# A norm's root moved behind the input products of a two-layer mixer, and the turn of rows by column halves

## Chip, cores and metric

The kernel runs on one core of a Trainium2 chip. The metric is the device time of one execution in microseconds (us), lower is better; 0.2% is 4 us.

## The reference, cut to what matters

Two blocks follow each other on 256 tokens of width 1024, all in float32. The first (layer norms, a state space mixer with attention, a mixture of 16 experts) ends in a layer norm with gain and bias. The second has two layers, and each of them begins so:

```python
def rmsnorm(x, g):
    x32 = x.astype(jnp.float32)
    y = x32 * lax.rsqrt(jnp.mean(x32 * x32, axis=-1, keepdims=True) + NORM_EPS)
    return (y * g.astype(jnp.float32)).astype(x.dtype)
...
# in each layer: h = rmsnorm(x, norm_mix); proj = h @ w_in  (2744 columns for
# three kinds of attention, then 3072 for the gates, which pass a sigmoid)
# ... attention, gates, products, cross attention, x = x + ...
# then x = x + w_down(silu(gate) * up), the feed-forward part with 2816 columns
```

The factor of the root is one number for each token, so it can be applied to the normed row or to the row of the product; both give the same `h @ w_in`.

## The kernel before, in words

Tokens lie on the 128 partitions in two blocks (`TB` = 2), `x_rows` holds them. A product needs its left side turned, so 128x128 tiles are transposed by TensorE (PE) with an identity into two PSUM banks X and O, two tiles `k` of two token blocks in one bank (`turn_rows`, L577; the transpose is L586). Most weights are used at a higher precision than one pass gives: a value is split into a rounded high part and a low part, and a product is made of three passes, high by high, high by low and low by high (`passes`, L599). For a chunk of weights ScalarE (ACT) writes the high part (`make_high`, L1346, the copy is L1353) and VectorE (DVE) subtracts it in place (`make_low`, L1665, L1669). For the turned tiles ACT writes the high part with the norm's gain (`turned_high`, L1355, L1362), and DVE writes the whole tile `h_t` (L1655), which the gate products read, and the low part (L1657).

All weights come through a ring of three places in SBUF (`SLOTS` = 3, a place holds 2 MB). SyncE (SP) issues the loads in the order of `LAYER_CHUNKS` (`load`, L1179, the issue is L1202); chunk number j goes to place j mod 3, and its load waits until PE has used the chunk before it in that place. A layer has 41 chunks and one `unused` behind them. It begins with `in1, in0, in2, in3, in4, in5` (the columns of the attention part; `in1` has 256 columns, `in4` and `in5` 476, the others 512), then the gates `g0` to `g5` among others; it ends with `gu0` to `gu10` (feed-forward, gate and up) and `fd0` to `fd5` (down; `fd5` is half a chunk). `in0` and `in2` are loaded in 16 pieces each, since their columns are put in another order on the way (pairs of heads, `PAIRED`).

The order of work is written by hand for each engine and held together by semaphores; each engine runs its own program in order. At the start of a layer:

```python
rms_rows("layer", "mix", ...)         # DVE: var, wait for GpSimd's root, x_rows * root -> h_rows (L1674, L1677)
turn_rows("mix", [... h_rows ...])    # PE: 8 tiles, two banks, so tiles 4 to 7 wait for 0 to 3
for i in IN_ORDER:                    # PE: product of both token blocks, banks G0 and G1
    product_rows("layer", f"in{i}", ...)
```

ACT computes the sums of squares for it (`square_rows`, L1341, two 128x1024 operations) as soon as `x_rows` is whole, GpSimd (POOL) takes the root (L1288), DVE scales the rows. ACT takes each product out of PSUM (`take`, L1331, L1339) into `proj`. DVE rotates the queries and keys (L2199 to L2209).

The turn into layer 0 comes behind the last product of the experts: DVE adds, norms and scales the rows (L2021, L1684 to L1701, the last two are the gain and the bias of the layer norm on 128x2048), and then the start above follows. The turn into layer 1 comes behind `fd5` of layer 0: PE's down product (L1128) runs over k, for each k over token block and column half, so both banks S and PT are full only at its end; DVE adds half of them to `x_rows` (L2456, two of 128x1024). At the start of each layer ACT issues eleven small loads (gains, position vectors, sinks, L1497 to L1502), PE turns the gains onto the partitions (L948) and DVE copies them (L2181).

## Time and profile before

| | |
|---|---|
| three runs | 1970.43, 1973.97, 1972.98 us; median 1972.98 |
| profiled execution | 1971.96 us, its span 1970.2 us |
| PE busy | 1755.8 us (89%), mean granted clock 0.932 |
| DVE, ACT, POOL busy | 853.9, 593.7, 22.6 us (43, 30, 1%) |
| DMA | 333.24 MB, mean 169 GB/s |

The profile is of one execution. A granted clock of 1.00 is 2.4 GHz, one of 0.50 is 1.2 GHz. `Ln` is a line of the kernel before. `ring_r`, `early_w` and `late_w` are the low part and the high parts of weights, `mix_high` and `mix_low` those of the turned tiles. "issue" in a chain is time in which an engine waited for nothing that the profile shows. The end of a row is its start plus its duration.

### The profile page before, as it was taken

What the parts mean: (1) busy time and instruction counts of PE and PEld (TensorE: products, weight loads), DVE (VectorE), ACT (ScalarE), POOL (GpSimd) and SP (SyncE); (2) the same over time, 40 slices, a digit from 0 to 9 for tenths busy, and PEclk for the clock granted to TensorE, in tenths of its full rate; (3) what the DMA queues carried; (4) which work ended last, traced back from release to release, by engine and by line L of the source; (5) the groups of instructions that cost most, each with busy time, mean ns of one, the idle gap of its engine ahead of it and who ended that gap; (6) DMA issues with size and microseconds to landing.
All of it is one profiled execution on the core that took longest, in us unless ns stands there. A gap on an engine that the chain in (4) does not pass through costs nothing.

```text
span 1970.2 us, 21742 instructions
## 1 busy us (share of the span) xinstructions
PE 1755.8 (89%) x9183; PEld 1284.4 (65%) x9183; DVE 853.9 (43%) x1201; ACT 593.7 (30%) x879; POOL 22.6 (1%) x80
## 2 busy tenths in 40 slices
PE   5999899988999959999988779996999989859997
PEld 1997555454434328565677679985756667649995
DVE  4675153243101055353465345534543365434643
ACT  1443210000111123243434234423333533433341
POOL 1000010000000000000000000000000000000000
PEclk9899787988999979999989889997999998979998
DMA  7455222657999964413234135536433232414552
GB/s 242 170 179 201 91 86 85 219 193 292 400 401 405 405 137 165 152 44 128 107 128 171 43 129 172 204 118 151 167 107 110 99 140 105 167 43 154 189 178 90
DMA packets 211212, 333.24 MB, mean 169 GB/s; under 512 B 51251, under 2 KB 102709, under 8 KB 211125
## 3 DMA queue, kind: packets, MB, share of 16 engines
q1 hardware_dynamic: 205312, 325.90, 47.5%
q10 hardware_dynamic: 5814, 6.11, 0.9%
q8 instruction: 65, 1.06, 0.2%
q14 instruction: 21, 0.17, 0.0%
HBM read 330.94 MB, written 1.05 MB: 168 GB/s over the span
## 4 chain that ended last, share of the span: by engine, by line
PE 68%; issue 12%; DVE 8%; DMA 7%; ACT 4%; SPq 1%; POOL 0%; POOLq 0%; DVEq 0%; ACTq 0%
PE ps_g L611 20%; PE ps_g L626 12%; PE ps_g L991 7%; DMA arena<-in_w_up_dram 5%; PE ps_g L911 4%; PE ps_o L681 3%; PE ps_p L611 2%; PE ps_s L611 2%; DMA ring<-in_w_mod_dram 2%; PE ps_p L1128 2%; PE ps_s L1128 2%; PE ps_s L652 1%; DVE ring_r L1669 1%; PE ps_x L586 1%; PE ps_p L671 1%
## 5 line engine op out<-in xcount | busy, mean ns | idle before, releaser
L1669 DVE TENSOR_TENSOR ring_r<-ring,late_w 128x4096 fp32r<-128x4096 f32 (+1 forms) x52 | 225.8, 4343 | 153.5 <-ACT late_w L1353 153.5
L1353 ACT ACTIVATE late_w<-ring 128x4096 fp32r<-128x4096 f32 (+1 forms) x52 | 185.0, 3557 | 234.7 <-PE ps_g L626 111.5
L626 PE MATMUL ps_g<-h_t_r,late_w 128*128 128x256 f32 x768 | 219.0, 285 | 0.0
L626 PE MATMUL ps_g<-hf_high,late_w 128*128 128x256 f32 x704 | 199.0, 283 | 3.8 <-DVE h_t_r L1657 3.8
L626 PE MATMUL ps_g<-hf_high,ring_r 128*128 128x256 f32 x704 | 199.0, 283 | 0.0
L626 PEld LDWEIGHTS ps_g<-h_t_r,late_w 128*128 128x128 f32 x768 | 148.6, 193 | 0.0
L991 PE MATMUL ps_g<-ring,h_t 128*128 128x512 f32 x320 | 145.7, 600 | 0.0
L626 PEld LDWEIGHTS ps_g<-hf_high,late_w 128*128 128x128 f32 x704 | 135.1, 192 | 4.5 <-DVE h_t_r L1657 4.5
L626 PEld LDWEIGHTS ps_g<-hf_high,ring_r 128*128 128x128 f32 x704 | 134.8, 192 | 0.0
L911 PE MATMUL ps_g<-ring,arena 128*64 128x512 f32 x384 | 115.7, 602 | 10.4 <-DMA arena<-in_w_up_dram 8.8
L1339 ACT ACTIVATE arena<-ps_g 128x512 f32<-128x512 f32 (+2 forms) x62 | 35.2, 567 | 219.3 <-PE ps_g L611 145.3
L991 PEld LDWEIGHTS ps_g<-ring,h_t 128*128 128x128 f32 x320 | 58.2, 190 | 63.9 <-issue 62.7
L611 PE MATMUL ps_g<-ring,h_t 128*128 128x512 f32 (+1 forms) x224 | 92.7, 573 | 5.0 <-DVE arena L2031 3.0
L911 PEld LDWEIGHTS ps_g<-ring,arena 128*64 128x64 f32 x384 | 36.5, 139 | 84.1 <-issue 84.1
L1377 ACT ACTIVATE arena<-arena,neg_max 128x256 f32<-128x256 f32 (+1 forms) x160 | 71.3, 448 | 61.0 <-DVE neg_max L1720 61.0
L586 PE MATMUL ps_x<-ident,h_rows 128*128 128x128 f32 x80 | 18.8, 379 | 73.1 <-DVE h_rows L1677 31.5
L611 PE MATMUL ps_g<-ring,arena 128*128 128x512 f32 (+1 forms) x176 | 75.3, 589 | 2.7 <-issue 1.6
L611 PE MATMUL ps_g<-early_w,mix_high 128*128 128x512 f32 (+2 forms) x192 | 72.9, 380 | 5.0 <-issue 5.0
L611 PEld LDWEIGHTS ps_g<-ring,h_t 128*128 128x128 f32 x224 | 43.7, 214 | 49.9 <-issue 48.6
L611 PE MATMUL ps_g<-ring_r,mix_high 128*128 128x512 f32 (+2 forms) x192 | 72.5, 378 | 0.0
L611 PE MATMUL ps_g<-early_w,mix_low 128*128 128x512 f32 (+2 forms) x192 | 72.2, 376 | 0.0
L681 PEld LDWEIGHTS ps_o<-arena 128*128 128x128 f32 x400 | 54.7, 211 | 26.3 <-issue 26.3
(525 smaller groups left out, 3366.6 us busy)
## 6 DMA issues: line engine op xcount, KB each, us to landing
ring<-in_w_in_dram SPq DMA_DIRECT2D x27, 2048.0 KB, 7.8
ring<-in_w_gate_up_dram SPq DMA_DIRECT2D x44, 1024.0 KB, 6.9
ring<-in_w_gate_dram SPq DMA_DIRECT2D x16, 2048.0 KB, 16.5
arena<-in_w_down_dram SPq DMA_DIRECT2D x16, 2048.0 KB, 15.3
ring<-in_w_mod_dram SPq DMA_DIRECT2D x12, 2048.0 KB, 9.4
ring<-in_w_down_dram SPq DMA_DIRECT2D x10, 2048.0 KB, 7.7
ring<-in_w_up_dram SPq DMA_DIRECT2D x8, 2048.0 KB, 18.0
arena<-in_w_up_dram SPq DMA_DIRECT2D x8, 2048.0 KB, 19.3
```

What stands on the lines that cost most here:

```text
L586: ins = pe.transpose(b.ap[0:size, i * SEQ + tb * P:i * SEQ + (tb + 1) * P], piece(tb), ident[:, :])
L611: ins = pe.matmul(b.ap[:, 0:n], x[:, k, tb * P:(tb + 1) * P], a[:, k, lo:lo + n], start=k == 0 and i == 0, stop=k == nk - 1 and i == len(b ...
L626: ins = pe.matmul(b.ap[:, (f % 2) * SEQ:(f % 2 + 1) * SEQ], a[:, k, f * P:(f + 1) * P], x[:, k, :], start=k == 0 and i == 0, stop=k == nk ...
L652: ins = pe.matmul(s4[:, i, 0:nk], q[lo:lo + HD, pair, qb * P:(qb + 1) * P], kk[lo:lo + HD, kpair, 0:nk], start=True, stop=kind != "fox")
L681: ins = pe.matmul(O.ap[:, i * width:(i + 1) * width], probs_t[:, i, b, :], v(step, i, b), start=b == 0, stop=b == kbs - 1)
L911: ins = pe.matmul(b.ap[lanes, :], taken_t[:, k, lanes], w[:, k, :], start=k == 0, stop=k == KD - 1)
L991: ins = pe.matmul(G[tb].ap[:, :], h_t[:, k, tb * P:(tb + 1) * P], w[:, k, :], start=k == 0, stop=k == KD - 1)
L1128: ins = pe.matmul(b.ap[:, half * HALF:(half + 1) * HALF], a[:, k, tb * P:(tb + 1) * P], x[:, k - 4 * c, half * HALF:(half + 1) * HALF], st ...
L1339: act.activation(d, src, func, scale=scale).then_inc(b.free, 1)
L1353: act.activation(high_w[name][:, 0:n], ring[:, slot, 0:n], ACT.Copy).then_inc(high_ready.sem, 1)
L1377: ins = act.activation(s, s, ACT.Exp, bias=neg_max[:, n % 2, i:i + 1], scale=-1.0, accum_out=den[:, n % 4, i:i + 1])
L1669: dve.tensor_tensor(ring_r[:, slot, 0:n], ring[:, slot, 0:n], high_w[name][:, 0:n].bitcast(F32), ALU.subtract).then_inc(low_ready.sem, 1)
```

## The change

1. The tiles for the input products are turned from `x_rows`, not from normed rows. The root goes to `mix_scale` (with half of it beside it for the gates), and ACT applies it as it takes the input products and the gate products out of PSUM. The rows are not scaled any more; `rows["mix"]` is gone. The squares run after the tiles' high copies.
2. The turn goes by column halves. The layer norm ahead of layer 0 gives `x_rows` in two halves; in the feed-forward part `fd5` goes by column half, then token block, and DVE adds half by half. PE turns tiles 0 to 3 on the first half (in the turn into layer 1 before the last group of `fd5`), and the first input product uses k 0 to 3, then the tiles 4 to 7 are turned between its two token blocks, then k 4 to 7 follow.
3. Layer 1 takes `in0` first, then `in1`; layer 0 keeps `in1, in0`. The ring's places stay those of `in1, in0, in2, ...` in both layers. `unused` moves ahead of `fd5`, and `in0` of layer 1 is loaded before `fd5`; its high and low parts are made behind those of `fd5`.
4. `in0` and `in2` are loaded whole; ACT writes their columns in the other order as it takes them.
5. `in1` uses the banks S and PT. The eleven small loads and the columns of gains are made earlier (for layer 0 ahead of the experts and in the layer norm, for layer 1 behind the tiles of `gu0`).

The diff, cut to its core:

```diff
-IN_ORDER = [1, 0, 2, 3, 4, 5]
+IN_ORDERS = ([1, 0, 2, 3, 4, 5], [0, 1, 2, 3, 4, 5])
...
-PIECES = {"in0": 2 * KD, "in2": 2 * KD, "dtf": 2, ...}
-PARTS = {..., "layer": (LAYERS, LAYER_CHUNKS + ["unused"])}
+PIECES = {"dtf": 2, ...}
+PARTS = {..., "layer": (LAYERS, LAYER_CHUNKS[:-1] + ["unused"] + LAYER_CHUNKS[-1:])}
...
-        ASIDE = ("bra1", "brb1", "brc1", "out1", "memv", "xo1")
+        ASIDE = ("in1", "bra1", "brb1", "brc1", "out1", "memv", "xo1")
...
             for l in range(LAYERS):
-                claim(X, "g_col", l)
...
-                pe.wait_ge(rows.sem, rows.at("layer", "mix", l))
-                turn_rows("mix", [lambda tb, k=k: h_rows[:, tb, k * P:(k + 1) * P] for k in range(KD)], l)
-                turned("layer", "mix", 4, l)
-                for i in IN_ORDER:
-                    n = IN_AT[i + 1] - IN_AT[i]
-                    product_rows("layer", f"in{i}", f"in{i}", (mix_high, mix_low), split_chunk(f"in{i}", KD, n, l), KD, 0, n, l)
+                if l == 0:
+                    gain_columns(0)
+                    for r in range(2):
+                        mix_rows(0, r)
+                for at_i, i in enumerate(IN_ORDERS[l]):
+                    name, n = f"in{i}", IN_AT[i + 1] - IN_AT[i]
+                    w = split_chunk(name, KD, n, l)
+                    if at_i:
+                        product_rows("layer", name, name, (mix_high, mix_low), w, KD, 0, n, l)
+                        continue
+                    for kh in range(2):
+                        for j, b in enumerate((X, O)):
+                            pe.wait_ge(b.free, b.nth("layer", f"mix{2 * kh + j}", l))
+                        for tb, b in enumerate(banks_of("layer", name)):
...
+                            for k in range(kh * KD // 2, (kh + 1) * KD // 2):
...
+                            if kh == 1:
+                                ins.then_inc(b.full, 1)
+                            elif tb == 0:
+                                for r in range(2, 4):
+                                    mix_rows(l, r)
...
+                w = split_chunk("fd5", KFF - 20, D, l)
+                pe.wait_ge(ff_low_ready, (l + 1) * (KFF // 2))
+                for half in range(2):
+                    for tb in range(TB):
+                        for k in range(20, KFF):
+                            ins = down(k, tb, half, w, 5)
+                        ins.then_inc((S, PT)[tb].full if half else ffd_part, 1)
+                        if half == 1 and tb == 0 and l + 1 < LAYERS:
+                            for r in range(2):
+                                mix_rows(l + 1, r)
...
                 for name in LAYER_CHUNKS:
+                    if (name, rnd) == ("in0", 1):
+                        continue
+                    if name == "fd5" and rnd + 1 < LAYERS:
+                        load("layer", "in0", rnd + 1)
                     load("layer", name, rnd)
...
-                make_high("in1", l, (last_used, l + 1))
-                act.wait_ge(x_ready.sem, x_ready.start["layer"] + l)
-                square_rows("layer", "mix", lambda tb: x_rows[:, tb, :], lambda tb: h_rows[:, tb, :], l)
-                make_high("in0", l)
-                act.wait_ge(g_col_ready, l + 1)
-                turned_high("mix", KD, mix_high, l, g_col[:, G_MIX:])
-                for at_i, i in enumerate(IN_ORDER):
-                    take("layer", f"in{i}", lambda tb, a=IN_AT[i], b=IN_AT[i + 1]: proj[:, tb, a:b], rnd=l)
-                    if at_i < 4:
-                        make_high(f"in{IN_ORDER[at_i + 2]}", l, done(f"in{i}"))
+                if l == 0:
+                    make_high("in1", l, (last_used, 1))
+                    make_high("in0", l)
+                    act.wait_ge(g_col_ready, 1)
+                    turned_high("mix", KD // 2, mix_high, l, g_col[:, G_MIX:])
+                turned_high("mix", KD, mix_high, l, g_col[:, G_MIX:], KD // 2)
...
+                square_rows("layer", "mix", lambda tb: x_rows[:, tb, :], lambda tb: rope_tmp[:, 0, tb * D:(tb + 1) * D], l)
+                if l:
+                    make_high("in1", l)
+                make_high("in2", l)
+                act.wait_ge(rstd_ready.sem, rstd_ready.at("layer", "mix", l))
...
+                for at_i, i in enumerate(IN_ORDERS[l]):
+                    take_in(i)
+                    if 1 <= at_i < 4:
+                        make_high(f"in{at_i + 2}", l, done(f"in{(0, 2, 3)[at_i - 1]}"))
...
+                if l + 1 < LAYERS:
+                    make_high("in0", l + 1)
+                    act.wait_ge(g_col_ready, l + 2)
+                    turned_high("mix", KD // 2, mix_high, l + 1, g_col[:, G_MIX:])
...
             for l in range(LAYERS):
...
-                rms_rows("layer", "mix", D, RMS_EPS, lambda tb: x_rows[:, tb, :], lambda tb: h_rows[:, tb, :], l).then_inc(rows.sem, 1)
...
-                make_low("in1", rnd=l)
-                turned_low("mix", KD, mix_low, mix_high, l, g_col[:, G_MIX:], h_t)
-                make_low("in0", rnd=l)
+                if l == 0:
+                    make_low("in1", rnd=l)
+                    mix_low_part(l, 0)
+                    mix_low_part(l, 1)
+                mix_low_part(l, 2)
+                mix_low_part(l, 3)
+                dve.wait_ge(squares.sem, squares.at("layer", "mix", l))
+                dve.tensor_scalar(var_in[:, :], square_sum[:, :], 1.0 / D, RMS_EPS, ALU.mult, ALU.add).then_inc(var_ready.sem, 1)
+                make_low("in1" if l else "in0", rnd=l)
+                dve.wait_ge(rstd_ready.sem, rstd_ready.at("layer", "mix", l))
+                dve.tensor_scalar(mix_scale[:, 1, :], mix_scale[:, 0, :], 0.5, None, ALU.mult).then_inc(mix_half, 1)
                 make_low("in2", rnd=l)
                 make_low("in3", rnd=l)
...
-                for tb, b in enumerate((S, PT)):
-                    x = x_rows[:, tb, :]
-                    dve.wait_ge(b.full, b.nth("layer", "ffd", l))
-                    dve.scalar_tensor_tensor(x, b.ap[:, :], 0.5, x, ALU.mult, ALU.add).then_inc(b.free, 1)
+                if l + 1 < LAYERS:
+                    make_low("in0", rnd=l + 1)
+                for half in range(2):
+                    for tb, b in enumerate((S, PT)):
+                        x = x_rows[:, tb, half * HALF:(half + 1) * HALF]
...
+                    if half == 0 and l + 1 < LAYERS:
+                        mix_low_part(l + 1, 0)
...
+                if l + 1 < LAYERS:
+                    mix_low_part(l + 1, 1)
```

`mix_rows(l, r)` waits for the half that holds tiles 2r and 2r + 1 and turns them into X or O; `mix_low_part(l, r)` is `turned_low` for these two tiles; `gain_columns` is the turning of the gains; `take_in` takes with `scale=mix_scale[:, 0, :]`, and for `in0` and `in2` into a permuted view of `proj`.

## Rows read from the trace of the kernel before

**Rows 1.** The page: shares of the chain that ended last, by engine.
```profile
PE 68%; issue 12%; DVE 8%; DMA 7%; ACT 4%; SPq 1%; POOL 0%; POOLq 0%; DVEq 0%; ACTq 0%
```

**Rows 2.** Chain of waits, 690 to 750: start, duration (us), engine, tile, line.
```profile
709.44 1.73 PE ps_p L876 x4
...
720.22 2.30 DVE x_rows L1699
...
724.87 1.15 ACT h_rows L1343 x2
...
733.15 1.13 PE ps_x L586 x4
...
735.17 0.69 DVE h_t L1655
735.86 0.79 DVE mix_low L1657 x2
...
738.13 11.98 PE ps_g L611 x68
```

**Rows 3.** Chain of waits, 1330 to 1362.
```profile
1334.81 1.41 PE ps_p L1128 x6
...
1344.34 3.60 DMA ring<-in_w_in_dram
...
1358.85 3.33 PE ps_g L611 x14
```

**Rows 4.** Timeline of DVE: start, duration, line, operation; in brackets idle time before.
```profile
1272.25 0.68 DVE L2442 SCALAR_TENSOR_TENSOR arena<-arena,ps_g 128x512 f32<-128x512 f32 x1
...
1336.24 1.23 DVE L2456 SCALAR_TENSOR_TENSOR x_rows<-ps_p,x_rows 128x1024 f32<-128x1024 f32 x1 [0.17 <-PE ps_p L1128]
...
1342.69 2.29 DVE L1669 TENSOR_TENSOR ring_r<-ring,early_w 128x2048 fp32r<-128x2048 f32 x1
...
1381.79 4.43 DVE L1669 TENSOR_TENSOR ring_r<-ring,early_w 128x4096 fp32r<-128x4096 f32 x1 [6.96 <-ACT early_w L1353]
...
1389.59 1.56 DVE L2209 TENSOR_TENSOR arena<-arena 128x640 f32<-128x640 f32 x2
```

**Rows 5.** Timeline of PE around 745.
```profile
745.32 0.40 PE L611 MATMUL ps_g<-early_w,mix_high 128*128 128x512 f32 x1
```

**Rows 6.** Timeline of ACT, 1130 to 1380 (ACTq is its queue of DMA issues).
```profile
1157.15 0.60 ACT L1615 ACTIVATE arena<-ps_g 128x512 f32<-128x512 f32 x1 [9.51 <-PE ps_g L626]
...
1308.38 3.63 ACT L1353 ACTIVATE late_w<-ring 128x4096 fp32r<-128x4096 f32 x1 [7.51 <-PE ps_p L1128]
1319.57 1.92 ACT L1353 ACTIVATE late_w<-ring 128x2048 fp32r<-128x2048 f32 x1 [7.56 <-PE ps_p L1128]
...
1323.40 0.61 ACTq L1502 DMA_DIRECT2D w<-in_nsa_wv_dram  x1
...
1366.46 0.39 ACT L1339 ACTIVATE arena<-ps_g 128x256 f32<-128x256 f32 x1 [2.44 <-PE ps_g L611]
...
1377.65 0.60 ACT L1339 ACTIVATE arena<-ps_g 128x512 f32<-128x512 f32 x1 [5.00 <-PE ps_g L611]
```

**Rows 7.** DMA issues, 1300 to 1450: count, size, us from issue to landing.
```profile
ring<-in_w_down_dram SPq DMA_DIRECT2D x1, 1024.0 KB, 4.9
```

**Rows 8.** Stretches: us, busy PE, PEld, DVE, ACT, POOL, granted clock, DMA, GB/s.
```profile
1336.20:1342.80 6.60, 0.07 (x2) 0.00 (x0) 3.44 (x10) 3.99 (x5) 0.69 (x1) 0.69 0.89 177
1358.80:1362.00 3.20, 3.15 (x15) 3.19 (x16) 3.20 (x1) 0.00 (x0) 0.00 (x0) 0.50 0.00 0
...
1371.00:1372.00 1.00, 1.00 (x6) 0.82 (x5) 1.00 (x1) 0.00 (x0) 0.00 (x0) 1.00 1.03 401
1373.00:1374.00 1.00, 1.00 (x6) 0.80 (x5) 1.00 (x1) 0.00 (x0) 0.00 (x0) 1.00 0.40 143
...
1434.50:1436.80 2.30, 1.39 (x12) 0.94 (x10) 1.65 (x3) 0.60 (x1) 0.00 (x0) 1.00 0.50 93
```

**Rows 9.** ACT's groups by form: line, operation, count, busy us, mean ns.
```profile
L1362 ACT ACTIVATE mix_high<-ps_x,g_col 128x256 fp32r<-128x256 f32 x8 | 3.3, 469 | 4.1 <-PE ps_x L586 4.1
```

More of the change, by code:

```diff
@@ L229 @@
 ARENA = 31100
-PIECES = {"in0": 2 * KD, "in2": 2 * KD, "dtf": 2, "cmp": 2, **{f"gu{i}": 2 for i in range(KFF // 2)}}
-PARTS = {"first": (1, FIRST_CHUNKS), "layer": (LAYERS, LAYER_CHUNKS + ["unused"])}
+PIECES = {"dtf": 2, "cmp": 2, **{f"gu{i}": 2 for i in range(KFF // 2)}}
+PARTS = {"first": (1, FIRST_CHUNKS), "layer": (LAYERS, LAYER_CHUNKS[:-1] + ["unused"] + LAYER_CHUNKS[-1:])}
 assert len(PARTS["layer"][1]) % SLOTS == 0
@@ L451, in two_blocks @@
         late_places = view_r("late_w0", 0, SLOT), view_r("late_w1", LAT_AT, SLOT)
-        high_w = {name: (early_places if name.startswith("in") else late_places)[i % 2] for i, name in enumerate(SPLIT)}
+        early_small = view_r("early_w2", QT_AT - 2816, SLOT // 2)
+        high_w = {name: late_places[i % 2] for i, name in enumerate(SPLIT)}
+        for rnd in range(LAYERS):
+            first, second = early_places if rnd == 0 else early_places[::-1]
+            high_w.update({(name, rnd): place for name, place in (("in0", first), ("in1", early_small), ("in2", second), ("in3", first),
+                                                                  ("in4", second), ("in5", first))})
         first_places = view_r("first_w0", S_AT - 2048, SLOT), view_r("first_w1", 0, SLOT)
@@ L1175, in sources @@
                 return [cols(t[w][rnd], lo, n)]
-            PAIRED = ("in0", "in2")
             def load(part, name, rnd=0):
@@ L1191, in load @@
                     dsts = [dst[:, 0], dst[:, 1]]
-                elif part == "layer" and name in PAIRED:
-                    dst = ring[:, slot, :].rearrange("p (k r f d) -> p k f r d", k=KD, f=2, d=HD)
-                    src = pieces[0].rearrange("p k (f r d) -> p k f r d", f=2, d=HD)
-                    dsts, pieces = ([v[:, k, f] for k in range(KD) for f in range(2)] for v in (dst, src))
                 else:
@@ L1646, in gain_turned, with turned_low @@
                                       over(gains[:, 2 * r:2 * r + n], SEQ), ALU.mult).then_inc(b.free, 1)
-            def turned_low(tag, tiles, dst, high, rnd, gains=None, whole=None):
-                for k in range(tiles):
+            def turned_low(tag, tiles, dst, high, rnd, gains=None, whole=None, start=0):
+                for k in range(start, tiles):
                     b, i = (X, O)[k // 2 % 2], k % 2
```

189 lines of the change are left out of this document (127 added, 62 removed).

## The prediction, before the change was run

> **What bounds the kernel now.** I read the page first: of the chain that ended last in the 1970.2 us span, work of TensorE (PE) is 68% [rows 1]. So a change pays only where PE stands still. Next I read the chain of waits at the two places that the change rewrites. From the last MoE product to the first input product of layer 0, PE has almost nothing to do: 709.44 + 1.73 = 711.17 to 738.13, 27 us, passed from VectorE (DVE) to ScalarE (ACT), GpSimd, DVE and PE and back [rows 2]. From the last down product of layer 0 (1336.22) to the first input product of layer 1 (1358.85) it is 22.6 us [rows 3]. There the chain runs through the sixteen pieces in which `in0` is loaded (the last one landed at 1347.94), then ACT's high copy, the turned tiles and DVE's low parts. Everything after each place is a stream of products in which PE hardly waits, so a shift of its start reaches the end.
>
> 0.2% of the time, 4 us, is about what a measurement can tell from no change.
>
> **Part 1, the turn into layer 0.** Removed from the path: the squares (from 724.87, two of 1.1 us), the variance and root, and the two scalings of rows [rows 2]. Added: the shift and scale run by halves. The full 128x2048 operation takes 2.30 us and starts at 720.22; one of 128x1024 takes 1.23 [rows 2, 4]. Four of 1.2: half 0 ready at 722.7, half 1 at 725.1. PE turns half 0 at once (two pairs of tiles at 1.1 each, half clock): 724.7. ACT's copies (0.84 per pair) follow till 725.5, hidden. DVE comes free at 725.1, makes `in1`'s low part (2.29, [rows 4]) and four tiles (0.69 + 0.79 per pair, overlapping by 0.1, [rows 2]): 730.2. PE starts `in1`'s first half there: 12 products of 256 columns at 0.21, 2.6 (0.118 at full clock, half of the 0.233 per 512 columns below; the slow clock is near double); two pairs of tiles 2.0; 12 products warm or cold, 1.4 to 2.6. The last tiles wait for ACT and DVE and are ready at about 737.5; the remaining 24 products at 0.118 end at 740.4 (at half clock 742.6). But `in0` needs its low part, and DVE stands behind the moved squares: ACT copies the last tiles until 735.5, squares until 737.6, DVE forms the variance and subtracts until 737.7 + 4.4 = 742.2. `in0` started at 745.32 [rows 5]. **Gain 3.1 us**, between 2.7 and 3.1: the last value whether `in1` ends at 740.4 or 742.6 hardly matters, since both lie near 742.2.
>
> The eleven small loads that ACT issues here moved ahead of the MoE loop; they are finished there long before they are needed. In the other turn they stand behind the copies of `hf`, where ACT has 9.5 us of idle time before its first tanh; before they followed the high copy of fd5, from 1319.6 to 1324.0, 4.4 us of issues [rows 6]. Cost nothing; if that cover were gone, 4.4 us. The transpose of the gains is only moved.
>
> **Part 2, the turn into layer 1.** The ring's order is changed: `in0` is loaded once fd2 is used (1308.3), whole, and lands 7.5 us later; fd5 waits for fd3 (1319.5) and lands at 1324.4 by a 1 MB load of 4.9 us [rows 7], high copy 1.92, low 2.29 [rows 4, 6]: ready 1328.6, needed 1330.6 (1336.22 less 24 products of 0.233). So fd5 stays hidden with 2 us to spare. ACT then copies `in0` (3.63) to 1329.9, DVE subtracts (4.43) to 1334.3 [rows 4, 6]. The first column half of the down product is done at 1333.4, but DVE is in that subtraction, so it adds half 0 only until 1335.6 (two at 0.68, [rows 4]). PE, after three of the four groups of fd5, waits from 1334.8 to 1335.7, turns four tiles (0.9) and finishes fd5 at 1338.0. DVE: tiles 0 and 1 to 1338.4, the two adds of half 1 to 1339.8, tiles 2 and 3 to 1341.3. PE idles 3.3 us and starts `in0` at 1341.3.
>
> Does the clock hold? In the 6.6 us after the last down product the mean granted clock is 0.69, so it fell from 2.4 to 1.2 GHz some 2.5 us in, and the first 3.2 us of the products ran at 0.50 and only then rose [rows 8]. After 3.3 us idle I take the fall, and 3.3 us at half clock again. Then: first half of block 0 to 1345.6, four tiles turned to 1346.5, block 1 to 1349.3; the tiles 6 and 7 are through ACT and DVE at 1349.7; 24 products at 0.233 (a 512 column block of weights, 48 products, takes from 1366.46 to 1377.65 between the last takes, [rows 6]) end at 1355.3. `in1`: squares till 1349.9, its high copy (1.91) till 1351.8, low 2.3 till 1354.1: in time. Its 48 products take 5.7: 1361.0. Before, `in2` began at about 1377.3, 0.4 ahead of that take. **Gain so far 16.3 us** (17.9 if the clock holds).
>
> What is late next: layer 1 now takes `in0` before `in1`, yet `in3` still goes into the ring place of `in1`. It can be issued only at 1361.0. A 2 MB load issued at 1366.05, when `in1` was done, moved data until 1373.4, 7.4 us [rows 8]; high 3.63, low 4.43: `in3` is ready at 1361.0 + 0.1 + 7.4 + 3.6 + 4.4 = 1376.5. `in2` covers only 11.2, to 1372.2. PE stands 4.3 us, the clock falls, and 3.3 us at half clock cost 1.6: **minus 5.9 us**. Before, `in1` came first and two products (22.4 us) covered this. After it, `in4` is not late: DVE's rotation takes from the end of a low part at 1386.1 to 1391.15 [rows 4], 5.0, plus at most 4.43 for the next low part, against 11.2 of `in3`.
>
> So turn 2 is worth 16.3 - 5.9 = **10.4 us**.
>
> The Trainium skill (TensorE: Matmul & The Clock Gate, section "HAM oscillation — how this bites in real kernels") says that a wait for weights between bursts of products makes each next burst start on the slow clock. By that rule the stall before `in3` costs 5.9, without it 4.3; the trace of before has no such stall in this stretch, only the two turns, where it agrees.
>
> **Part 3, the end.** DVE's last add is a half block: 0.68 for 1.23 [rows 4]. **Gain 0.55 us.**
>
> **Part 4, evictions.** The takes of `in` and of the gates read their factor from memory. A 128x256 copy with such a factor takes 0.47, one without 0.39 [rows 6, 9], the first writing another type as well. 0.08 on some 24 takes a layer, beside products: 1.9 us of ACT's time in each layer, so a cost between 0 and 3.8 us; I take 0, as ACT idles 5.0 us before a typical take [rows 6]. The permuted write of `in0` and `in2` has no row; the nearest are copies of the same 512 columns, 0.60 [rows 6], and it lies beside 11 us of products: 0, and at most another 0.6 each. The sixteen pieces become one load: a gain already in the sum.
>
> **Sum.** 3.1 + 10.4 + 0.55 = 14.0. The profiled execution took 1971.96 (1.8 around its span), so 1957.9; it lies 1.0 under the median of the three runs. I give 1958.
>
> **The rivals.**
> *A, no stall before `in3`.* The load lands sooner, or the copy chain overlaps more than I think. Then 14.0 + 5.9 = 19.9, and 1952. For: nothing in the rows but the small spread of the loads. Against: three durations in series that all have rows. 0.12.
> *B, `in3` shares the queue.* `in4` (place of `in0`, free since 1355.3) is issued right behind `in3`. If both share the engines evenly, 4 MB at about 400 GB/s [rows 8] take 10.5 us and `in3` lands some 3 to 5 us later: 1961 to 1963. Against: a queue that works in order. 0.12.
> *C, slower: the clock does not come back.* The new turns are bursts with waits of 1 to 4 us between them (1334.8, 1338.0, 1372.2 and, in layer 0, 735.8, 740.4). If PE stays at 1.2 GHz through `in1`, `in2` and `in3` of layer 1, their 28.1 us at full clock double: 14.0 - 28.1 = 14 us lost, 1986. It decides from about 28 us of further half clock on, where the gain is eaten. Against: after both turns full clock came back after 3 to 4 us of work, and in a stretch where PE is busy 1.39 of 2.30 us the clock is 1.00 [rows 8]. 0.05.
> The Trainium skill (same page, "A second HAM failure mode: psum-queue depth-cycling") tells of just that, short idles between groups that change banks and a clock that falls again and again; the trace of before speaks against it with the clock of 1.00 beside such idles.
> *D, nothing.* Another chain, such as fd5's, whose load now starts 11 us later with only 2 us to spare, or ACT's longer queue, eats the gain in the same place: 1969 to 1975. 0.06.
>
> **How the numbers follow.** Forecast 0.65 with its own range 1955 to 1961; A 0.12, B 0.12, C 0.05, D 0.06. 1951 to 1964 takes in A and B and leaves out C and D and the tails of the rest. Faster by over 4 us: 0.92 (forecast, A, B and part of D); within 4 us 0.03; slower 0.05.
>
> **What would show it.** In the profile after: `in0` of layer 0 starts near 742 (745.32 before); PE works between 730 and 738; the squares come after the tiles. In layer 1, shifted by the 3 us of the first turn: down product to first input product some 5 us instead of 22.6; a wait of DVE on ACT's copy of `in3` that reaches back to the load, with PE idle about 4 us before `in3`'s products and a clock of 0.50 after it. If there is no such gap, A holds. If PE stands before fd5, D. If the stretches from `in1` to `in3` show 0.50, C. The prediction is wrong if the first product of layer 1 starts more than 3 us away from 1341 minus the shift.

## The result, and the profile after

The changed kernel takes **1957.74 us** (median of 4 runs, 1956.37 to 1959.55); the kernel before, beside it, 1972.69 (4 runs, 1970.43 to 1973.97). The ratio is 0.9926, interval 0.991 to 0.9941: 15 us faster, forecast 1958.0. The profiled execution took 1956.37 us. Its page, the first line and the chain's shares by engine (68% PE before, [rows 1]):

```profile
span 1954.4 us, 21694 instructions
PE 66%; issue 12%; DVE 9%; DMA 8%; ACT 4%; POOL 0%; SPq 0%; POOLq 0%; DVEq 0%; ACTq 0%
```

Chain of waits of the changed kernel, turn into layer 0, from the root of the layer norm ahead of it on (answers to [rows 2]):

```profile
717.23 0.74 POOL rstd L1349
...
719.57 1.24 DVE x_rows L1792
...
724.45 2.20 DVE ring_r L1762
...
729.67 2.90 PE ps_s L996 x12
732.57 0.87 PE ps_x L973 x4
...
733.46 0.84 ACT mix_high L1425 x2
...
735.15 1.03 ACT arena L1406 x2
...
737.43 4.34 DVE ring_r L1762
741.76 0.04 issue
741.81 4.21 PE ps_g L624 x17
```

No second root stands between the shifted rows and the tiles any more. The column tiles come first, then the squares (735.15), then `in0`'s low part (737.43), and PE starts `in0` when that ends, at 741.81 (745.32 before, [rows 5]). The chain names the squares ahead of the low part, but VectorE's own last column tile ends at 737.19, when the squares end too (737.24), so either would hold the low part until then:

```profile
736.32 0.87 DVE L1750 SCALAR_TENSOR_TENSOR first_low<-ps_o,g_col,mix_high 128x256 fp32r<-128x256 f32 x2
```

The same view, turn into layer 1 (answers to [rows 3]):

```profile
1325.12 4.43 DVE ring_r L1762
1329.55 1.21 DVE x_rows L2576 x2
...
1330.80 0.67 PE ps_x L973 x4
...
1336.97 5.46 PE ps_g L996 x12
1342.43 0.48 PE ps_x L973 x4
...
1346.88 5.73 PE ps_g L996 x24
1352.61 2.81 PE ps_s L624 x24
1355.42 2.83 PE ps_p L624 x24
...
1358.26 7.77 DMA ring<-in_w_in_dram
...
1366.06 3.63 ACT early_w L1416
...
1369.71 4.44 DVE ring_r L1762
...
1374.19 2.08 PE ps_g L624 x4
```

The first product of layer 1 comes at 1336.97, some 4 us after the last down product, and not 22.6. Behind `in1`'s last product the chain runs through `in3`'s load, its high part and its low part: this is the new stall that was forecast. The clock in both waits (by stretch: us, PE, PEld, DVE, ACT, POOL busy, granted clock, DMA share, GB/s):

```profile
1334.00:1337.00 3.00, 0.03 (x1) 0.06 (x1) 2.57 (x5) 0.00 (x0) 0.00 (x0) 0.76 0.87 266
1337.00:1341.00 4.00, 4.00 (x10) 3.13 (x11) 0.00 (x0) 0.00 (x0) 0.00 (x0) 0.50 0.85 325
...
1372.00:1374.00 2.00, 0.00 (x0) 0.00 (x0) 2.00 (x1) 2.00 (x1) 0.00 (x0) 0.77 1.05 402
1374.00:1378.00 4.00, 3.81 (x9) 3.04 (x10) 3.93 (x10) 0.42 (x1) 0.00 (x0) 0.50 0.48 183
```

Where the 15.8 us lie by which the second profiled span is shorter (1970.2 and 1954.4), by the starts of the same operation in both:

| stretch, and the operation at its end | time before, after | gain in it | forecast |
|---|---|---|---|
| up to the end of the last MoE product | 711.17, 710.48 | 0.7 | 0 |
| turn into layer 0 (take of `in0`) | 756.62, 753.15 | 2.8 | 3.1 |
| rest of layer 0 (high copy in the down product) | 1297.23, 1292.63 | 1.1 | 0 |
| turn into layer 1 (take behind `in3`'s first block) | 1394.45, 1382.65 | 7.2 | 10.4 |
| rest of layer 1 (last down product) | 1957.04, 1941.73 | 3.5 | 0 |
| end (variance of the output norm) | 1961.07, 1945.23 | 0.5 | 0.55 |

So the three stretches that were costed gave 10.5 of 14.0 us, and 5.3 came from stretches for which the forecast had no term. The total was right partly by that, and this part was luck. The 4.6 us in the rest of the two layers are no waits of PE, which stands still there for 45.1 us in the kernel before and 45.2 and 45.1 in the changed one; most of them are granted clock. Two such stretches of the layers, each between the same two ScalarE operations (us, then busy time of PE, PEld, DVE, ACT, POOL, granted clock, DMA share, GB/s). The kernel before:

```profile
1051.81:1162.86 111.05, 81.99 (x442) 71.23 (x441) 44.71 (x46) 38.52 (x54) 1.38 (x2) 0.85 0.28 95
1612.83:1784.07 171.24, 133.07 (x700) 114.25 (x699) 81.51 (x82) 57.97 (x76) 2.07 (x3) 0.86 0.31 106
```

The changed kernel:

```profile
1048.12:1157.64 109.52, 80.47 (x443) 69.71 (x442) 45.01 (x46) 38.51 (x55) 1.38 (x2) 0.88 0.29 97
1600.80:1768.49 167.69, 129.46 (x700) 111.40 (x699) 81.33 (x82) 57.94 (x76) 2.07 (x3) 0.88 0.32 109
```

PE stands still for 29.06 and 29.05 us in the first, for 38.17 and 38.23 in the second (the length less its busy time), yet the changed kernel is 1.5 and 3.6 us shorter.

### The profile page after: what moved, and what is told of

Read it like the earlier page. It is cut to its first block, busy times and chain, and to the rows that moved or that the text cites. A ratio compares the mean times of both kernels' runs of the same rounds, so it can differ in the third digit from the quotient of the medians.

```text
span 1954.4 us, 21694 instructions
## 1 busy us (share of the span) xinstructions
PE 1748.7 (89%) x9183; PEld 1277.1 (65%) x9183; DVE 851.2 (44%) x1205; ACT 597.3 (31%) x879; POOL 26.7 (1%) x80
## 4 chain that ended last, share of the span: by engine, by line
PE 66%; issue 12%; DVE 9%; DMA 8%; ACT 4%; POOL 0%; SPq 0%; POOLq 0%; DVEq 0%; ACTq 0%
PE ps_g L624 18%; PE ps_g L639 12%; PE ps_g L1040 7%; DMA arena<-in_w_up_dram 5%; PE ps_g L924 4%; PE ps_o L694 3%; DVE ring_r L1762 2%; PE ps_p L624 2%; PE ps_s L624 2%; DMA ring<-in_w_mod_dram 2%; PE ps_s L665 2%; PE ps_x L599 1%; PE ps_p L684 1%; PE ps_g L726 1%; PE ps_p L1175 1%
## 5 line engine op out<-in xcount | busy, mean ns | idle before, releaser
L1762 DVE TENSOR_TENSOR ring_r<-ring,early_w 128x4096 fp32r<-128x4096 f32 (+2 forms) x12 | 47.6, 3968 | 45.2 <-ACT early_w L1416 45.2
L694 PE MATMUL ps_o<-arena 128*128 128x64 f32 (+1 forms) x400 | 53.5, 289 | 13.1 <-ACT arena L1453 13.1
L924 PE MATMUL ps_g<-arena 128*64 128x512 f32 x128 | 62.9, 649 | 0.0
L624 PE MATMUL ps_g<-early_w,mix_high 128*128 128x512 f32 (+1 forms) x144 | 57.0, 396 | 6.3 <-DVE ring_r L1762 6.3
L1762 DVE TENSOR_TENSOR ring_r<-ring,first_w 128x4096 fp32r<-128x4096 f32 x11 | 48.7, 4425 | 27.5 <-ACT first_w L1416 27.5
```

What stands on the lines that cost most here:

```text
L624: ins = pe.matmul(b.ap[:, 0:n], x[:, k, tb * P:(tb + 1) * P], a[:, k, lo:lo + n], start=k == 0 and i == 0, stop=k == nk - 1 and i == len(b ...
L694: ins = pe.matmul(O.ap[:, i * width:(i + 1) * width], probs_t[:, i, b, :], v(step, i, b), start=b == 0, stop=b == kbs - 1)
L924: ins = pe.matmul(b.ap[lanes, :], taken_t[:, k, lanes], w[:, k, :], start=k == 0, stop=k == KD - 1)
L1762: dve.tensor_tensor(ring_r[:, slot, 0:n], ring[:, slot, 0:n], high_of(name, rnd)[:, 0:n].bitcast(F32), ALU.subtract).then_inc(low_ready.se ...
```

## The experiments

Each is an edit of the changed kernel. They ran in three groups of four, each with the kernel before beside it:

| run | median (runs) | ratio to before, interval |
|---|---|---|
| e1_places | 1956.27 (4) | 0.993, 0.9905 to 0.9955 |
| e2_busy | 1965.43 (10) | 0.9969, 0.9955 to 0.9984 |
| e3_low_early | 1957.97 (5) | 0.9943, 0.9922 to 0.9963 |
| e5_whole_rows | 1958.83 (6) | 0.9943, 0.9926 to 0.9959 |
| before beside these | 1970.93 (16) | |
| e6_fill | 1958.53 (10) | 0.9943, 0.9923 to 0.9963 |
| e7_in0_first | 1956.31 (10) | 0.9938, 0.9915 to 0.996 |
| e8_norm_path | 1970.71 (10) | 1.0006, 0.9991 to 1.0022 |
| e9_load_late | 1961.72 (10) | 0.9974, 0.9954 to 0.9995 |
| before beside these | 1969.77 (31) | |
| e10_best | 1945.94 (4) | 0.9871, 0.9856 to 0.9887 |
| e11_best_fill | 1947.2 (4) | 0.9881, 0.9863 to 0.9899 |
| e4_plain | 1961.67 (3) | 0.9951, 0.9926 to 0.9975 |
| a0_again (the changed kernel) | 1958.48 (5) | 0.9935, 0.9921 to 0.9949 |
| before beside these | 1969.6 (10) | |

Runs of one kernel lie up to 15 us apart (e7_in0_first, 1950.22 to 1965.06), and the profiled executions enter the first turn between 1.7 us earlier and 8.8 us later than the changed kernel's, by what they lost in the part ahead of it, which all share. A few us can't be read from the medians. So each edit is also read in its own stretch: the start of the same operation ahead of the stretch and behind it, against the first profile of the changed kernel (**shift**, minus is earlier).

**e1_places: what holds `in3` back**

```diff
-            slot, count, per = PLACE[part, name]
+            slot, count, per = place_of(part, name, rnd)
```

(`place_of` gives `in3` and `in4` each other's place in layer 1.)

> Edit: in layer 1 alone, in3 and in4 swap their places in the ring of the low parts, so that in3's load waits for in0's last product and not for in1's. Theory (the stall before in3 is the load that in1's place holds back, 4.9 us of idle PE in the changed kernel's trace, and the products behind it start at the low clock, some 1.6 us): in3's load is issued at the end of in0, 5.6 us earlier, in3's products follow in2's with under 0.5 us between, and the time falls by 5.0 to 6.5 us against the changed kernel, to 1951 to 1953 us. Then in4 takes in1's place and must be there at in3's end, which it is with 4 us to spare. Rival (the stall is the scalar and vector engines' own pace in making the parts, not the load): both in3's parts come no more than 1 us earlier, since the two engines stand in a queue behind in2's parts, and the time falls by under 1.5 us.

Shift 4.4 ahead of the turn, 4.4 at `in0`, -3.5 behind `in3`: **7.9 us gained**, by theory 5.0 to 6.5. `in3`'s low part (vector engine) is made at 1368.35, and with the shift of 4.4 that is 5.8 us earlier than in the changed kernel; its products follow `in2`'s without a wait, at full clock:

```profile
1368.35 4.43 DVE L1770 TENSOR_TENSOR ring_r<-ring,early_w 128x4096 fp32r<-128x4096 f32 x1 [7.60 <-ACT early_w L1424]
...
1374.00:1378.00 4.00, 4.00 (x19) 3.30 (x18) 3.93 (x8) 3.66 (x2) 0.00 (x0) 1.00 0.76 258
```

Up to `in3`'s first product 5.1 us were gained (shift -0.7 there; the wait was 4.9), and the half clock behind it was worth another 2.8. The rival is out. But at the end of the program the shift is -0.3: of 7.9 us, 3.1 were given back between 1620 and 1770, which this edit does not touch. PE stands still there as long as in the changed kernel (38.24 us); the granted clock is lower, as in the kernel before:

```profile
1597.34:1768.18 170.84, 132.60 (x700) 114.02 (x699) 81.51 (x82) 57.95 (x77) 2.07 (x3) 0.86 0.31 107
```

**e2_busy and e6_fill: is it idling that drops the clock, and what does that cost?**

```diff
+                    if l == 1 and i in (0, 3):
+                        for _ in range(8 if i == 0 else 11):
+                            pe.matmul(d.ap[:, 0:SEQ], ident[:, :], tri[:, :], start=True, stop=True)
```

(`d` is bank G0 ahead of `in0` and S ahead of `in3`; in e2_busy there are 16 and 21.)

> Edit: at the turn into layer 1 PE runs products that nobody reads, 16 in the 3.7 us in which it waits for in0's first column tiles and 21 in the 4.9 us in which it waits for in3's parts, each 128 x 128 by 256 columns in fp32 and some 0.21 us. No work of the kernel is changed. Theory (the two half-clock spells behind these waits, 0.50 from 1337 to 1341 us and from 1374 to 1378 us, are there because PE idled, and each costs 1.6 to 1.9 us): the granted clock stays at 1.00 in both places, in0's first 12 products take 2.7 us and not 5.5, and the time falls by 2 to 4 us against the changed kernel, less 0.2 to 0.5 us for products that run over the wait. Rival (the clock falls for another reason than idling, or the time that it costs is hidden behind the parts that the scalar and vector engines make): the clock is 1.00 yet the time is within 1 us of the changed kernel's, since in3 waits for its load from in1's end and the first spell's gain comes back only as far as in1 ends earlier; or the clock is still 0.50.

> Edit: as in e2_busy, PE runs products that nobody reads in the two waits of the turn into layer 1, now 8 and 11 of them. In e2_busy one of them took 0.42 us, not the 0.21 that was reckoned with (each fp32 product is two passes), so 16 and 21 ran 3 and 4 us over the waits; the clock stayed at 1.00. Theory (a half-clock spell behind each wait costs 2.4 to 2.8 us, and idling of PE is its cause): the fillers take 3.4 and 4.6 us and fit the waits of 3.7 and 4.9; the clock is 1.00 in both stretches, the shift against the changed kernel falls by 2 to 2.6 us at in0 and by as much again behind in3, together 4 to 5 us. Rival (the clock falls in any case when only such fillers run, or the fillers hold up the real products by as much): the shift changes by under 1.5 us in all.

In e2_busy the clock was 1.00, but the fillers ran over both waits: they took twice the time that was reckoned (first row, 16 of them 7.07 us). The edit cost about 2 us in the turn (shift 10.5 ahead, 12.3 behind) and can't give the price. e6_fill does (second and third row):

```profile
1343.54 7.07 PE L991 MATMUL ps_g<-tri,ident 128*128 128x256 f32 x32
```

```profile
1332.78 3.61 PE L991 MATMUL ps_g<-tri,ident 128*128 128x256 f32 x16
1336.63 0.47 PE L1004 MATMUL ps_g<-early_w,mix_high 128*128 128x512 f32 x1 [0.23 <-DVE first_low L1758]
```

Shift -0.3 ahead and at `in0`'s first product, -2.8 behind its first 12 products, -2.5 at `in3`'s first product, **-5.2** behind it: 4.8 us gained. With PE busy the clock stays at 1.00 in both places, and the two half-clock spells cost 2.5 and 2.7 us. The theory stands for these two waits. Later, between 1620 and 1770, 1.6 us are given back.

Idling is not the only thing that a fall can follow. From 850 to 905 PE never waits, in the changed kernel or in e5_whole_rows, and runs the same products: small ones of 16 columns, then these eight. In the changed kernel, timeline of PE and stretch:

```profile
881.34 5.40 PE L1040 MATMUL ps_g<-ring,h_t 128*128 128x512 f32 x8
882.00:884.00 2.00, 2.00 (x4) 0.80 (x3) 0.91 (x5) 0.31 (x1) 0.00 (x0) 0.50 0.00 0
```

In e5_whole_rows, which is 8.5 us later here:

```profile
889.80 3.70 PE L1040 MATMUL ps_g<-ring,h_t 128*128 128x512 f32 x8
890.50:892.50 2.00, 2.00 (x6) 0.80 (x6) 0.87 (x5) 0.31 (x1) 0.00 (x0) 1.00 0.00 0
```

The same eight products take 1.7 us longer in one of them. Why the clock falls here is open.

**e3_low_early: what sets `in0`'s start in layer 0**

```diff
                     mix_low_part(l, 1)
+                    make_low("in0", rnd=l)
...
-                make_low("in1" if l else "in0", rnd=l)
+                if l: make_low("in1", rnd=l)
```

> Edit: at the turn into layer 0 the vector engine makes in0's low part (4.42 us) in the 4.9 us in which it stands idle between its column tiles, and not behind the variance of the rows. Theory (in0's start at 741.8 us in the changed kernel is set by in0's low part behind the squares, and nothing else is late there): the products of in0 start when both the column tiles and the low part are there, at 739.5 to 740.5 us, and the time falls by 1.2 to 2.0 us. The reciprocal root on GpSimd, 4.8 us long while the vector engine makes the low part in the changed kernel, is back at 0.7 us. Rival (the low part is not what ends the wait: the scalar engine's column tiles and squares, or in1's takes, are): in0 starts within 0.5 us of 741.8 and the time is the same.

Shift -1.7 ahead, -3.5 behind (`in0`'s take): **1.7 us gained**, as forecast. The low part runs in the vector engine's idle time, `in0` starts at 738.49 (740.1 without the edit, by the shift), and the root takes 0.69 us (below, 4.79 in the changed kernel):

```profile
727.61 4.42 DVE L1762 TENSOR_TENSOR ring_r<-ring,early_w 128x4096 fp32r<-128x4096 f32 x1
735.66 0.69 POOL L1349 TENSOR_TENSOR mix_scale<-var_in,half_power 128x2 f32<-128x2 f32 x1 [19.42 <-DVE var_in L2296]
738.49 0.39 PE L624 MATMUL ps_g<-early_w,mix_high 128*128 128x512 f32 x1
```

**e5_whole_rows: what the column halves bring**

```diff
-                        if half == 1 and tb == 0 and l + 1 < LAYERS:
-                            for r in range(2):
-                                mix_rows(l + 1, r)
...
+                if l + 1 < LAYERS:
+                    for r in range(2):
+                        mix_rows(l + 1, r)
```

(The second place is behind the last product of fd5. With it, `mix_rows` waits for both halves in both layers, and DVE's four additions come ahead of all column tiles.)

> Edit: the turn by column halves is undone, the rest of the change kept: at both turns PE turns rows only once the whole row tiles are there (at the turn into layer 1 behind the last product of fd5), and the vector engine makes its column tiles behind all four additions. The norm's reciprocal root stays at the evictions. Theory (the gain of the turn comes from the norm's leaving the path, and the halves bring only what runs early, some 1 us in each turn): in0 starts 0.5 to 2 us later in each turn than in the changed kernel, and the time rises by 1 to 3 us, to 1959 to 1961 us, still 11 to 14 us under the kernel before. Rival (the halves carry a large part of the gain): the time rises by 5 us or more, since both halves' tiles then stand behind the last addition and PE idles over 5 us longer.

Shift 8.6 ahead of the first turn, 8.6 behind its first tiles (8.46 at `in0`'s take); 10.6 ahead of the second, 10.5 at `in0`'s first product, 10.7 behind `in3`. **Turning and adding by column halves brings nothing**, in either turn. The rival falls, and so does my 1 us. Two parts of the halves stay in this run and were not tested: the first product still goes by k 0 to 3 and 4 to 7, and the layer norm still gives its rows in halves. In the first turn PE turns the first rows 2.4 us later (11.0), and it is absorbed: VectorE makes `in1`'s low part first in both kernels and comes to the tiles at the same time. In the second:

```profile
1342.77 0.66 PE L973 MATMUL ps_x<-ident,x_rows 128*128 128x128 f32 x4 [0.83 <-DVEq L2585]
...
1347.50 0.77 PE L996 MATMUL ps_g<-early_w,mix_high 128*128 128x512 f32 x1 [3.64 <-DVE first_low L1750]
```

PE waits as long before `in0` (3.64 and 3.69), because VectorE has the same four additions and four column tiles to do behind `in0`'s low part, in another order.

**e8_norm_path: what the norm cost on the path**

```diff
+            def scale_rows(l):
+                ...
+                for tb in range(TB):
+                    ins = dve.tensor_scalar(rope_tmp[:, 0, tb * D:(tb + 1) * D], x_rows[:, tb, :], mix_scale[:, 0, tb:tb + 1], None, ALU.mult)
+                ins.then_inc(mix_scaled, 1)
```

(e5_whole_rows with this, which DVE runs ahead of the tiles of both layers, behind the variance and a wait for the root; `mix_rows` on PE waits for `mix_scaled`, and ACT's squares move ahead of its column tiles.)

> Edit: e5_whole_rows (no column halves), and the norm is put back on the path of both turns: squares, variance, root and two multiplications of 128 x 1024 rows run before PE may turn the rows. Their product is written aside, so that all results stay those of the changed kernel; the evictions still apply the factor. Against e5_whole_rows: Theory (the gain of 2.8 us in the turn into layer 0 and a part of that in the turn into layer 1 is the norm's leaving the path): in0 starts 2.5 to 4 us later in layer 0, where the squares no longer stand between the tiles and in0's low part, and 4 to 6 us later in layer 1 (squares 2.3, variance, root and waits 1.2, rows 1.4). Time 6 to 10 us up. Rival (in layer 1 the early load of in0 carries all of the gain, and the norm's chain would be hidden behind fd5's and in0's parts): under 1 us in layer 1.

Against e5_whole_rows: **4.7 us in the first turn** (0.1 ahead, 4.8 behind). Ahead of the second only 0.3 are left in PE's products (most of the rest went between 1027 and 1158), then 6.0 at `in0`'s first product, 4.9 behind its first half and 4.4 behind `in3`: **4.1 us in the second turn**. The theory stands. In layer 0 it was a little more than expected: moving the squares ahead gave nothing back, since `in0`'s low part still stands behind VectorE's last column tile. In layer 1 `in0` was 5.7 us late, as expected, and shorter half-clock spells than e5_whole_rows has took 1.6 off. By the ratios (1.0006 and 0.9943) the norm costs 12 us, more than the two stretches show, and all of the change's gain, though the early load is still in: as said, the medians also hold what the other stretches give and take. This run is not the old turn: at `in0`'s take in layer 0 it has lost 4.5 us to the changed kernel since entering the turn, the kernel before 2.8. PE's wait:

```profile
1348.29 1.12 PE L974 MATMUL ps_x<-ident,x_rows 128*128 128x128 f32 x4 [6.03 <-DVE arena L2294]
```

**e9_load_late: what the early load of `in0` brings**

```diff
-                    if name == "fd5" and rnd + 1 < LAYERS:
-                        load("layer", "in0", rnd + 1)
                     load("layer", name, rnd)
+                    if name == "fd5" and rnd + 1 < LAYERS:
+                        load("layer", "in0", rnd + 1)
```

> Edit: in the SP queue in0 of layer 1 is loaded behind fd5, not ahead of it; nothing else is changed. Theory (the early load carries a part of the gain in the turn into layer 1): fd5 is no longer late-bound on the queue; in0's load starts when fd5's is issued, at 1314.8 us or a little later, lands some 7.5 us behind fd5's, near 1327, then 3.62 for the high and 4.43 for the low part: 1335.2 where the changed kernel has 1329.5. So the additions and all that follows come 5 to 6 us later, and so does the end. Rival (in0's place in the ring is free so early that the order on the queue changes nothing, as PE's own work ends at 1333): under 1 us.

Shift -0.3 ahead (in PE's down products), 3.5 at `in0`'s high part, 4.5 at its first product, 3.4 behind `in3`: **3.7 us lost**. The theory's sign stands, its size was some 2 us too high: I had put the two loads in series (4.9 + 7.5), but queued behind fd5's the 2 MB load landed 10.0 us after its issue (issues of e9_load_late, 1310 to 1325: KB each, median us to landing), 4.9 behind fd5's 5.1 and not 7.7:

```profile
ring<-in_w_in_dram SPq DMA_DIRECT2D x1, 2048.0 KB, 10.0
ring<-in_w_down_dram SPq DMA_DIRECT2D x1, 1024.0 KB, 5.1
```

Set against e8_norm_path, this does not make up the second turn. Its 7.2 us are what is left beside a stall that took 7.9 (e1_places), so some 15 us have to be explained. The norm (4.1) and the load ahead of `fd5`'s (3.7) are half of them. The other half was not taken apart: in the kernel before, `in0` was issued in sixteen pieces, and only behind the last down product [rows 3], while in e9_load_late it is still issued over 20 us ahead of that product (at 1314.91), whole.

**e7_in0_first: the 0.80 us before the turned columns**

```diff
                 for c in range(2, 6):
+                    if c == 5 and l + 1 < LAYERS: make_low("in0", rnd=l + 1)
                     make_low(f"fd{c}", rnd=l)
-                if l + 1 < LAYERS: make_low("in0", rnd=l + 1)
```

> Edit: at the turn into layer 1 the scalar and vector engines make in0's high and low parts ahead of fd5's, not behind them. Theory (the vector engine is in in0's low part until 1329.5 us, so it adds the first column half late and PE waits 0.80 us before it turns these columns; and the scalar engine idles 12.3 us before fd5's copy): in0's parts are made in that idle time, the first two additions start as soon as their products end, the 0.80 us of waiting before the turned columns goes, and in0's first product comes 0.8 to 1.5 us earlier relative to the last part of fd3. Rival (the wait is for the last products of fd5 and their additions, in any case): in0's start moves by under 0.3 us. It would be slower only if fd5's low part, now last, came later than its products want it (1330.6 us), which by the rows is 4 us away.

Shift 4.5 ahead, 3.5 at the turned columns (no wait there any more), 3.0 to 2.4 within `in0`, 1.8 behind `in3`: **2.7 us gained**, 1.0 by the wait and the rest by shorter half-clock spells.

**e4_plain: the dearer evictions.** It replaces `scale=mix_scale[...]` by 1.0 and 0.5, so it leaves the norm's root out of the result.

> Edit: the evictions of the input products and of the gates use the constants 1.0 and 0.5 for the norm's factor in memory; all waits stay. So the mixer norm's reciprocal root is left out of the computation. Theory (the dearer evictions lie beside products and cost nothing): a 128x512 eviction is back at 0.60 us from 0.69, and the stretch from in2 to the last gate shortens by under 0.3 us in each layer. Rival (each eviction holds its bank, so some 24 of them cost 0.09 us each on the path): 1.5 to 2.2 us a layer.

```profile
755.52 0.60 ACT L1402 ACTIVATE arena<-ps_g 128x512 f32<-128x512 f32 x1 [4.62 <-PE ps_g L624]
```

In the changed kernel the same eviction takes 0.69 (at 753.15, in the last section). Shift 7.9 ahead of layer 0's input products, 7.7 at 894 and 7.6 at 974; 7.6 ahead of layer 1's and 7.6 to 1500. **At most 0.3 us in layer 0, none in layer 1**: Part 4's zero stands.

**a0_again: the same kernel, a second profile**

> The changed kernel itself, unedited, for a second profile and more runs beside e10_best. Theory (the products behind the turns do the same work, and the shifts of 1 to 3 us that the two profiles show in the layers' later parts come from half-clock spells that fall elsewhere in every run): the two turns take what they took in the first profile to within 0.3 us, while the stretches with spells differ by 1 to 3 us; median 1955 to 1959 us, 12 to 16 us under the kernel before run beside it. Rival (the gain behind the turns is the change's own, by its cheaper stretches): the spells lie at the same places of the program as in the first profile.

From 45 us on the shift lies between 0.8 and 1.3 to the end: the turns repeat to 0.3 us, and so do the stretches with half-clock spells. My theory, that they fall elsewhere in every run, is wrong for these two, which entered alike; the rival's sign, the same places, came true. e5_whole_rows, which entered 8.6 later, has a shift of 6.8 at 888, 5.4 at 987 and 10.0 at 1083 in products that it shares with the changed kernel word for word. The fourteen profiles together say more. The stretch that lies at 753.74 to 1157.64 in the changed kernel takes 400.7 to 406.0 us in them, 405.8 in the kernel before, while PE waits 45.1 to 45.3 in each. The one at 1600.80 to 1768.49 takes 167.6 to 167.7 in the changed kernel, a0_again, e3_low_early, e4_plain and e5_whole_rows, 170.8 in e1_places and e11_best_fill and 171.2 in the kernel before, with 38.2 of waiting in each. Runs that enter a stretch alike take the same: e2_busy and e5_whole_rows enter layer 0 at 8.4 and 8.5 and both take 406.0. So what unchanged stretches take goes with the time at which they are entered, by up to 5 us, with the same waits and another granted clock. The 4.6 us that layers 0 and 1 gained behind the turns are of this size and show no shorter wait. That the change itself made no part of them is likely by this, but not shown, since there is one profile of the kernel before; the medians (11.1 us apart in this group, 15 in the first) say that a part of them comes and goes.

**e10_best and e11_best_fill: a version that beats both**

e10_best is e1_places, e3_low_early and e7_in0_first together; e11_best_fill adds the 8 fillers before `in0`.

> Edit: e1_places, e3_low_early and e7_in0_first together. Each alone gained in its own stretch, by the times at which the stretch was entered and left: 7.9, 1.8 and 2.6 us, of which 0.5 of the last was a warmer start of in3 that e1_places has already. Theory (the three lie in series): 11 to 12 us in the two stretches. Some of it is given back behind them, as after e1_places (from 7.9 us to 4.8 at the end, where half-clock spells of the layer's later part took more), so the time falls by 7 to 12 us against the changed kernel run beside it. Rival (they share one cause, or the spells of half clock eat them): under 4 us.

> Edit: e10_best with the 8 products that nobody reads in the wait before in0 of layer 1. Theory (the half-clock spell behind this wait costs 2.4 us, as e2_busy and e6_fill showed): clock 1.00 from the last down product to the end of in3, another 1.5 to 2.4 us less than e10_best. Rival: within 0.5 us of e10_best at the end of in3.

e10_best: 1945.94 us, **12.5 us under the changed kernel** beside it, and the intervals do not touch. Shift 8.8 ahead of the first turn, 7.1 behind; 4.1 ahead of the second, -5.9 behind and -6.0 at the end: 1.7 and 10.0 us, 11.7 as reckoned, and nothing was given back behind the second. In the second turn one cause of waiting is left, the column tiles (waits of PE, 1320 to 1385, total, times, longest):

```profile
PE ps_g L1004 <- DVE first_low L1760: 4.4, 2, 3.7
```

The fillers took 1.3 us off there (the shift between the two goes from -7.0 to -8.2), less than expected, as e10_best's spell was already shorter, and 3.4 were lost again between 1620 and 1770. By the medians e11_best_fill is no better.

## Why the prediction was right, and where it was not

**What bounds.** Right: in both turns PE stood, and 10.5 of the forecast 14.0 us came off in the stretches that were costed.

**Part 1, layer 0.** Forecast 3.1, measured 2.8. The step that set it, `in0`'s low part, is the one in the chain (737.43) and the one that e3_low_early removes. That it stood behind the moved squares is half of it: it stood behind VectorE's last column tile as well, which ends within 0.1 us of them, and in e8_norm_path, with the squares moved ahead, it begins right behind that tile. That half clock in `in1` does not matter was right too. What was not seen: turning by column halves adds nothing here (e5_whole_rows), while the norm, put back, costs 4.7, more than the turn gained.

**Part 2, layer 1.** The first product was due at 1341.3 in the time of before and came at 1336.97, 1341.6 with the 4.6 us that the program was ahead: 0.3 off. fd5 stayed hidden. The stall before `in3` came, for the reason given: load, high part and low part behind `in1`'s last product. Rival A falls with it. **What failed are two sizes.** First, the half clock after each wait: I took 3.3 us of it, 1.6 us of loss. All of `in0`'s first 12 products ran at half clock, 5.46 us for the 4.3 in the sum, and behind `in3` the shift to before fell by 2.7 (14.5 to 11.8). e6_fill prices the two spells at 2.5 and 2.7. Second, small ones: `in3`'s load 7.77 for 7.4, the middle of `in0` 0.5 late. Together 10.4 became 7.2.

The half clock was read from the stretch of before in which the first 3.2 us stood at 0.50 [rows 8]; that a spell can be longer was not reckoned with. By the rule of the Trainium skill that was cited (TensorE: Matmul & The Clock Gate, "HAM oscillation — how this bites in real kernels") every such wait restarts the products at the slow clock: here it did so at both, and e6_fill shows that products in the wait prevent it.

**Part 3** was 0.5 for 0.55. **Part 4** stands: a 128x512 eviction is 0.09 us dearer, e4_plain finds at most 0.3 us in one layer and nothing in the other.

**The rivals.** B falls: `in4`, issued right behind `in3`, did not delay it (7.77 us; ACT waited 0.22 us for `in4`'s landing). C falls: full clock was back within 6 us after each wait. D falls. The slower outcome had no support in any run.

**What I had no term for** is 0.7 ahead of the turns and 4.6 in the layers behind them. Without it the time would have been 1962 to 1963, inside the stated range of 1951 to 1964 but outside the 1955 to 1961 that the forecast gave itself. So the mechanisms were right, and that 1957.74 lies so near to 1958 is luck: terms that were 3.5 us too large in all and 5.3 us that were left out nearly cancel.

## What to carry to other kernels

When a step is taken off the path, ask for each engine in turn what it has queued: here the order of VectorE's own work decided that starting PE earlier, by column halves, was worth nothing, and a 4.4 us operation moved into VectorE's idle time was worth 1.7. When the order of tiles in a ring changes, look up who used each place last: one swapped pair of places was worth 7.9 us in its stretch. Read an edit of a few us in its stretch, at an operation ahead and one behind, and only then in the medians, since later stretches can give back or add as much.

## What the runs showed of the hardware

**A small GpSimd operation waits for a large VectorE one.** The root on 128x2 elements takes 0.73 us at 717.23, and 4.79 when it is issued just after VectorE began the subtraction of two 128x4096 tiles in SBUF. Changed kernel, timelines of ACT, POOL and DVE:

```profile
753.15 0.69 ACT L1402 ACTIVATE arena<-ps_g,mix_scale 128x512 f32<-128x512 f32 x1 [4.80 <-PE ps_g L624]
```

```profile
737.51 4.79 POOL L1349 TENSOR_TENSOR mix_scale<-var_in,half_power 128x2 f32<-128x2 f32 x1 [19.54 <-DVE var_in L2295]
```

```profile
737.34 4.42 DVE L1762 TENSOR_TENSOR ring_r<-ring,early_w 128x4096 fp32r<-128x4096 f32 x1
```

It ends 0.5 us behind the subtraction, and in e3_low_early, with VectorE idle, it takes 0.69. The Trainium skill (SBUF — State Buffer, section "Who interferes with whom") says that a VectorE instruction with two SBUF inputs contends with a GpSimd one that reads SBUF, and that this contention is an exclusive lock; the trace agrees, 6.9 times longer. Here `in1`'s evictions and VectorE's halving of the root waited for it, off the path.

**An fp32 product of 128x128 by 256 columns took 0.44 to 0.45 us**, two records each (7.07 us for 16 in e2_busy, 3.61 for 8 in e6_fill), twice the 0.21 that I had reckoned for e2_busy.

**Two loads in one queue**: 1 MB and 2 MB issued together landed at 5.1 and 10.0 us; alone the same 2 MB took 7.7. Adding the two durations would have given 12.8, which is 2.8 too much.

**Not tried**: why 24 of the input products' 512 column passes take 5.49 us now (takes at 753.15, 758.64) and 5.54 before (756.62, 762.16).
